# w_out of the first layer split inside the context hyena's stage, one core, Trainium2

## What is computed

```python
    o_ssd = _rms_norm(y_ssd.reshape(B, L, SSD_WIDTH) * jax.nn.silu(z)) * ssd_norm_w
    o_hy = _hyena(hp, hy_conv_w, hy_conv_b, hy_filt, hy_bias) * jax.nn.silu(gh)
    o = jnp.concatenate([o_ssd, o_diff, o_hy], axis=-1) @ w_out
    h_new = _layer_norm(ALPHA * h + gate * o) * ln_g + ln_b
    if not need_ctx:
        return h_new, None
```

## Time and profile before

| | us |
|---|---|
| median of 3 executions | 3879.47 (3876.34 to 3891.03) |
| the profiled execution: span from its first to its last instruction | 3883.2 |
| PE busy in it | 3384.6 (87%) |
| DVE busy | 2463.6 (63%) |
| ACT busy, POOL busy | 1091.4, 1069.9 (28% each) |

### The profile page before, as it was taken

One profiled execution on the slowest core, in us unless ns is written; L12 is line 12 of the kernel. 1 busy time (PEld: TensorE's weight loads), 2 busy tenths in 40 slices (PEclk: granted clock), 3 DMA queues, 4 the chain that ended last, 5 costly groups with the idle time before them and its releaser, 6 DMA issues. The chain is left out here.

```text
span 3883.2 us, 48582 instructions
## 1 busy us (share of the span) xinstructions
PE 3384.6 (87%) x18212; PEld 2751.0 (71%) x18212; DVE 2463.6 (63%) x4480; ACT 1091.4 (28%) x1981; POOL 1069.9 (28%) x782
## 2 busy tenths in 40 slices
PE   6999999999868886886997888999999588858798
PEld 2787888888767774554783677888888587745477
DVE  4134577755369996885564324557775599968765
ACT  2111222212245454332210211222211455523321
POOL 4233334333212222210122423433443022232121
PEclk8999999999989998998998999999999899979899
DMA  5254223223163222334526155323331733133442
GB/s 204 69 155 147 80 91 96 87 89 97 52 203 98 73 73 79 121 113 133 156 76 217 52 126 164 97 81 98 96 95 57 204 91 93 43 107 110 128 144 68
DMA packets 414893, 423.34 MB, mean 109 GB/s; under 512 B 57040, under 2 KB 351440, under 8 KB 413506
## 3 DMA queue, kind: packets, MB, share of 16 engines
...
## 5 line engine op out<-in xcount | busy, mean ns | idle before, releaser
L754 PE MATMUL l_p_acc<-l_u_hi,l_w_hi 128*128 128x512 f32 (+1 forms) x2208 | 607.3, 376 | 29.1 <-ACT l_p_stg L818 15.5
L754 PE MATMUL l_p_acc<-l_u_hi,l_w_lo 128*128 128x512 f32 (+1 forms) x2208 | 589.1, 368 | 0.0
L754 PE MATMUL l_p_acc<-l_u_lo,l_w_hi 128*128 128x512 f32 (+1 forms) x2208 | 587.5, 367 | 0.0
L754 PEld LDWEIGHTS l_p_acc<-l_u_hi,l_w_hi 128*128 128x128 f32 x2208 | 384.2, 190 | 106.6 <-issue 32.7
L667 POOL TENSOR_TENSOR l_w_hi<-l_wt,l_p_zero 128x1024 fp32r<-128x1024 f32 x100 | 203.8, 2038 | 906.0 <-PE l_p_acc L754 749.0
L754 PEld LDWEIGHTS l_p_acc<-l_u_hi,l_w_lo 128*128 128x128 f32 x2208 | 381.9, 189 | 72.2
L754 PEld LDWEIGHTS l_p_acc<-l_u_lo,l_w_hi 128*128 128x128 f32 x2208 | 381.7, 189 | 72.1
L1506 PE MATMUL l_at_pS<-l_at_k_hi,l_at_q 128*128 128x512 f32 (+1 forms) x400 | 165.8, 414 | 131.0 <-ACT l_at_prob L1622 75.3
L669 POOL TENSOR_TENSOR l_w_lo<-l_wt,l_w_hi 128x1024 fp32r<-128x1024 f32 x100 | 266.1, 2661 | 7.9
L2457 PE MATMUL l_o_pA<-l_o_w_hi,l_o_o_hi 128*128 128x512 f32 x576 | 224.5, 409 | 42.2 <-DVE l_o_o_lo L2567 31.8
L1740 DVE TENSOR_REDUCE l_at_nmax<-l_at_pS 128x1 f32<-128x1280 f32 (+1 forms) x144 | 197.2, 1370 | 96.8 <-PE l_at_pS L1507 92.6
...
## 6 DMA issues: line engine op xcount, KB each, us to landing
l_wt<-w_in SPq DMA_DIRECT2D x104, 512.0 KB, 3.9
...
l_o_rows<-w_out SPq DMA_DIRECT2D x32, 512.0 KB, 4.5
...
qk_d<-l_p_late ACTq DMA_DIRECT2D x12, 1280.0 KB, 4.6
```

The source lines that it names most:

```text
L754: mm = pe.matmul(acc[:, a:a + w], (w_hi, w_lo)[wp][m % 2][:, k], (u_hi, u_lo)[up][:, k, t0 + c:t0 + c + w], start=(k == n == 0), stop=(k = ...
```

## The change

hyena_stage also fetches, rounds and splits all 16 tiles of w_out, into w_hi and w_lo that outlive it and are handed to output_stage. It has four buffers raw; the tiles alternate between the rest (even n, split by POOL) and the SSD tiles (odd n, split by DVE with ssd_norm_w); ACT rounds all of them. Where each engine does this is written out by hand. In output_stage of the first layer the fetches, roundings and splits are gone, SP fetches the first two token tiles at once, and PE does all 16 blocks of tile 0 and then all of tile 1, with row_sums after blocks 3 and 7 of tile 0 and block 7 of tile 1. The second layer's output_stage runs as before. The buffer Tm of hyena_stage is halved; what lay in its other half was not used.

```diff
-def hyena_stage(nc, tag, J, tok0, ident, hp_d, kf_d, fwd_d, inv_d, o_d):
+def hyena_stage(nc, tag, J, tok0, ident, hp_d, kf_d, fwd_d, inv_d, o_d, w_out, norm_w, w_hi, w_lo):
...
+        w_order = [k for pair in zip(range(SSD_TILES, KM), range(SSD_TILES)) for k in pair]
+        raw = sb(nc, ctx, tag + "raw", [P, RAWS, D])
...
+                def load_w(i):
+                    k = w_order[i]
+                    if i >= RAWS:
+                        m = i - RAWS
+                        sp.wait_ge(ssd_split if m % 2 else rest_split, m // 2 + 1)
+                    sp.dma_start(raw[:, i % RAWS], w_out[k * P:(k + 1) * P]).then_inc(w_in[i % RAWS], 16)
+
+                for i in range(RAWS):
+                    load_w(i)
                 sp.wait_ge(tok_ready, 2 * J)
                 sp.dma_start(xg[:], rows(2 * HYW)).then_inc(x2_in, 16)
+                for i in range(RAWS, 8):
+                    load_w(i)
                 sp.wait_ge(y_ready, 2 * J)
                 sp.dma_start(K[:], kf_d[1]).then_inc(k_in[1], 16)
+                for i in range(8, KM):
+                    load_w(i)
...
+                rounds_before = {0: (0, 1), 2: (2, 3), 4: (4, 5, 6, 7), 6: (8, 9), 8: (10, 11, 12, 13, 14, 15)}
...
                 for i, (o, h, k) in enumerate(turns):
+                    for n in rounds_before.get(i, ()):
+                        round_w(n)
                     act.wait_ge(q_mm, i + 1)
...
+            @block.gpsimd
+            def _(pool):
+                for n in range(0, KM, 2):
+                    wk = w_order[n]
+                    pool.wait_ge(w_rounded, n + 1)
+                    pool.tensor_tensor(w_lo[:, wk], raw[:, n % RAWS], w_hi[:, wk], ALU.subtract).then_inc(rest_split, 1)
...
                 products(0, 0)
                 products(0, 1)
+                split(1)
+                split(3)
                 back(0, 0)
                 forth(1, 0)
                 back(0, 1)
                 forth(1, 1)
+                split(5)
+                split(7)
                 products(1, 0)
                 products(1, 1)
+                split(9)
                 back(1, 0)
+                split(11)
                 back(1, 1)
+                split(13)
+                split(15)
+                dve.wait_ge(ssd_split, KM // 2)
...
-                for n in range(KM + LEAD):
+                if w_split_before:
+                    for n in range(KM):
+                        block_of(0, n, (0, 1))
+                        if n in (3, 7):
+                            row_sums((3, 7).index(n))
+                    for n in range(KM):
+                        block_of(1, n, (0, 1))
+                        if n == 7:
+                            row_sums(2)
+                for n in range(KM + LEAD if not w_split_before else 0):
...
                 act.wait_ge(step, 1)
-                for n, k in enumerate(K_ORDER):
+                if w_split_before:
+                    round_rest(0)
+                    square(0)
+                    root_of(0)
+                    round_ssd(0)
+                    round_rest(1)
+                    square(1)
+                    root_of(1)
+                    round_ssd(1)
```

More of the change, by code:

```diff
@@ L2205, in hyena_stage @@
         R = sb(nc, ctx, tag + "R", [P, 2, J, 2, HALF])
[L2206 removed]
+        Tm = sb(nc, ctx, tag + "Tm", [P, 2, 8, HALF])
         K = sb(nc, ctx, tag + "K", [P, 2 * J + 1, HYW])
@@ L2378, in output_stage @@
         WS = len(w_in)
-        w_hi = sb(nc, ctx, tag + "w_hi", [P, KM, D], F32R)
-        w_lo = sb(nc, ctx, tag + "w_lo", [P, KM, D], F32R)
+        w_hi, w_lo = w_split_before or [sb(nc, ctx, tag + part, [P, KM, D], F32R) for part in ("w_hi", "w_lo")]
         rows = sb(nc, ctx, tag + "rows", [P, WS, D])
@@ L2412, in _ @@
                 sp.dma_start(oT[:, 0, SSD_TILES:], o_d[SSD_TILES * P:, t * P:(t + 1) * P].rearrange("(k p) t -> p k t", p=P)).then_inc(o_in[0], 16)
-                for n, k in enumerate(K_ORDER):
+                if w_split_before:
+                    sp.dma_start(oT[:, 0, 0:SSD_TILES], o_d[0:SSD_TILES * P, t * P:(t + 1) * P].rearrange("(k p) t -> p k t", p=P)).then_inc(first_in, 16)
+                    load_o(1)
+                for n, k in enumerate(K_ORDER if not w_split_before else []):
                     if n >= WS:
@@ L2451, in block_of @@
                         pe.wait_ge(ssd_split, i + 1)
-                    if i == 0:
+                    if i == 0 and not w_split_before:
                         pe.wait_ge(w_split, n + 1)
@@ L2580, in _ @@
                 dve.memset(mv[:, 0:1], RMS_EPS).then_inc(step, 1)
-                for n, k in enumerate(K_ORDER):
+                if w_split_before:
+                    split_rest(0)
+                    scale(0)
+                    split_ssd(0)
+                    split_rest(1)
+                    scale(1)
+                    split_ssd(1)
+                for n, k in enumerate(K_ORDER if not w_split_before else []):
                     if n == 1:
@@ L2698, in hybrid_backbone @@
                 ssd_stage(nc, g + "sd_", t0 // P, tri, ident, small, a["ssd_d"][layer], a["c_sel"], xbc_d, las_d, gate_z, o_d)
+            dst = h_d[CTX:T] if need_ctx else out[0]
+            with ExitStack() as octx:
+                w_split_before = None
                 if need_ctx:
[L2700 to L2703 removed]
+                    w_split_before = [sb(nc, octx, g + part, [P, KM, D], F32R) for part in ("wo_hi", "wo_lo")]
+                    hyena_stage(nc, g + "ctxh_", CT, 0, ident, hp_d, KF[CT], a["c_fwd_ctx"], a["c_inv_ctx"], o_d, a["w_out"][layer], a["ssd_norm_w"][layer], *w_split_before)
+                output_stage(nc, g + "o_", t0 // P, tri, o_d, a["w_out"][layer], a["ssd_norm_w"][layer], mod_d, a["ln_g"][layer], a["ln_b"][layer],
+                             h_lat, h_ctx, dst, h_d[0:CTX], w_split_before)
 INPUTS = ["x", "c", "ctx", "c_ctx", "w_ada", "b_ada", "w_in", "ssd_conv_w", "ssd_conv_b", "ssd_dt_bias", "ssd_a_log", "ssd_d",
```

33 lines of the change are left out of this document (24 added, 9 removed).

## The result

| | before | with the change |
|---|---|---|
| median of 20 executions each, us | 3879.60 (3867.07 to 3891.03) | 3890.16 (3878.24 to 3902.00) |
| profiled span, us | 3883.2 | 3892.2 |

A forecast was written before the change was run, and what follows sets the result against it. PE was taken to set the pace from tile 2 on, DVE's order the context hyena's end. Output stage -10.9, context hyena +15.2, barriers +1.35 made +5.7 us: 3888.9 on the profiled span, forecast 3885 since the median lies 3.7 lower; range 3872 to 3898.

The forecast's parts named there:

- the forecast's two terms: Output stage: PE stands 3.5 us at the second row sum, then loses 1.6 us to the lower clock.
- The term for the lower clock behind the stop: Output stage: after its new wait at the second row sum PE loses 1.6 us to the lower clock.
- Barriers: Between stages: three more barriers at 0.45 us each, plus 1.35 us.
- The fetches of the first four tiles ... nothing: Context hyena's start: w_out's first fetches, queued behind the inverse matrices, come before any engine wants them and cost nothing.
- Item 1: Context hyena, ahead of back(0, 0): DVE's splits 1 and 3, the latter waiting for ACT's fourth rounding, plus 3.4 us.
- Item 2: Context hyena, between back(0, 0) and the second products: DVE's splits 5 and 7, plus 2.6 us, K just covered.
- Items 3 and 4: Context hyena's end: splits 9 and 11, then the last tile's fetch, rounding and split; together plus 4.8 us.
- Item 5: Context hyena: three of POOL's eight subtractions slow DVE by 1.47 us each, plus 4.4 us, bounds 0 and 11.8.
- third rival: Context hyena, second convolution: DVE's splits leave PE idle, its transforms run at 1.2 GHz; plus 6 us, 3891, chance 0.1.
- POOL and DVE hold each other up: Context hyena: three to five stops of a whole subtraction, K late; 3 to 9 us on top, 3891, chance 0.17.
- The cover holds: Rival: POOL's work costs DVE nothing, PE isn't stopped at the second row sum; minus 3.9 us, 3875.6, chance 0.2.
- the change does not reach its aim: Rival: row sums, POOL and landings hold PE; the output stage gives back 4 us or less, 3892, chance 0.05.

The follow-up runs named there:

- e4_sums_later: The change with row_sums of token tile 1 moved from behind block 7 of tile 0 to behind block 11; ratio to before 1.0029.
- e2_pool_memset: The change with POOL writing zeros into w_lo of the eight rest tiles, reading nothing, in place of its subtractions; ratio to before 1.0017.
- e1_nw_late: The change with DVE's wait for ssd_norm_w moved from ahead of forth(0, 0) to just ahead of split 1; ratio to before 1.0030.
- e6_dve_memset: The change with DVE writing zeros into w_lo of the eight SSD tiles in place of its splits; ratio to before 1.0027.
- e3_all_dve: The change with DVE making the eight rest splits too, so POOL has no work in the context hyena; ratio to before 1.0025.
- e9_three: The change with all splits on DVE, the ssd_norm_w wait at its first use and tile 1's row_sums after block 11; ratio to before 1.0016.

## Why the prediction was right or wrong

The time, 3890.16 us, lies in the range (3872 to 3898) and in the case's own (3877 to 3892), and "within 0.5%" was right. The sum wasn't: +5.7 us was forecast, 12.4 measured. By stages it is 23.3 - 11.6 + 1.2 = 12.9. That the time fell in the range says little for the sum: the range is 26 us wide and takes in every rival. One of the forecast's own signs of being wrong came: the context hyena grew by more than 20 us. Of the signs of being right, DVE's gaps ahead of splits 3 and 9 came (0.93 and 2.01 us), the one ahead of split 15 didn't; that the output stage's first issue stands at "about 1832" (1831.54) is luck, since this execution was 8.85 us ahead and the stage 8.1 us longer than forecast.

**Output stage, right.** PE's start 6.47 us after the issue (forecast 6.6), row_sums of tile 0 at 13.5 (13.9), the new wait behind POOL 3.05 (3.5), tile 2 at 58.2 (58.9). e4_sums_later measured the wait with its clock loss at 4.7, where the forecast's two terms make 5.1. The term for the lower clock behind the stop was right for this execution (and for e2_pool_memset); in e1_nw_late and e6_dve_memset it was nothing, with a dearer start instead.

**Barriers, right**: 1.0 to 1.2 for 1.35.

**Context hyena, too small by 8.1 us.** By the stretches of e2_pool_memset, in which POOL blocks nothing (66.81 - 50.45 = 16.4 us), and the 7.0 us that POOL's reading adds:

- *"The fetches of the first four tiles ... nothing".* True for them, but the step left out a line of the diff: DVE's wait for ssd_norm_w ahead of forth(0, 0). The vector of 4 KB needed 9.4 us to land and held DVE back for 2.6 us (e1_nw_late).
- *Item 1* (3.4): 30.46 - 27.13 - 0.24 = 3.1 without the lock. Right.
- *Item 2* (2.6): (39.98 - 30.46) - (31.97 - 24.74) = 2.3. Right. K was covered by more than forecast: it was in at 1798.0, 5.1 us before DVE came to it, and the second products took 8.47 us, as before.
- *Items 3 and 4* (4.8): 16.92 - 10.01 = 6.9, 2.1 more than forecast. The last tile's fetch took 6.0 us to land there, where item 4 had 4.0. In the kernel of the change itself it took 3.7 and the tile was in 3.8 us after split 11, as assumed, and DVE, late by POOL, didn't wait for it.
- *Item 5* (4.4): a stop was priced too low (1.47 us, measured 1.8 in the mean), and they were counted too few: the trace of the change shows seven where I counted three. For the splits the code itself makes them meet: ACT rounds a pair of tiles, POOL starts on the first, and DVE comes to the second 1.0 us later (1787.06 and 1813.60). They are 12.7 us, of which 7.0 lengthen the stage and 5.7 lie where the fetches or PE would have made DVE wait anyway.
- The rest, 1.4 us, is the second products at PE's lower clock, as in the third rival. It stood in e2_pool_memset (9.91 instead of 8.47 us), e3_all_dve and e9_three, not in the kernel of the change, where the stops of POOL took its place.

These make 2.6 - 0.3 - 0.3 + 2.1 + (7.0 - 4.4) + 1.4 = 8.1. It is a way of sharing out the 8.1, by a kernel that isn't the change. In the change's own rows the stage grew by 2.7 up to the first products' end, 4.3 to back(0, 0), 6.5 to the second products, nothing in them and 9.9 behind them, and 1.2, 4.2 and 7.4 us of standing still lie in the second, third and last of these.

So what came to pass is the rival "POOL and DVE hold each other up", which I had priced at 3891 and given 0.17, with seven stops where it had three to five and without its late K, together with a wait that I missed. The rule of the Trainium skill ("SBUF — State Buffer", Who interferes with whom), by which a DVE instruction with two SBUF inputs and a GpSimd instruction that reads SBUF shut each other out for a whole instruction, agrees with the trace in three ways: DVE's 0.42 became 2.57 beside POOL's 2.52; products with one input in PSUM kept their length inside POOL's 2.36 (e1_nw_late); and beside a POOL that only writes none grew (e2_pool_memset). The forecast had the rows for it and took a middle value: by the rule the 1.63 us lost in two rows were what remained of POOL's work when DVE came, not a share of it. Its reading of the rule, 2.34 us for each stop, was too much in turn: a stop costs what remains, 1.2 to 2.2 us here.

"The cover holds" fails on POOL's stops, and "the change does not reach its aim" on the 11.6 us. The aim was reached; the place to which the work went cost twice that.
